# Both norms of a one-layer decoder trunk handed to TensorE chunk by chunk, with filler transposes and a first weight slot in halves

## The chip, the cores and the metric

The kernel runs on one core of one Trainium2 chip. The metric is the device time of a run in microseconds (us), the median of several runs. The engines are PE (TensorE: `MATMUL` and, as PEld, its weight loads), DVE (VectorE), ACT (ScalarE), POOL (GpSimd) and SP (SyncE, which here only issues DMAs). They run side by side, each through its own list of instructions in order, and meet only at semaphores.

## The reference

One layer on x, 256 tokens by 1024 channels, all float32:

```
h  = rmsnorm(x, norm1)                       # first norm
z  = h @ w_in                                # split into rx, ry, q, kc, vc, ks, vs, kw, vw, ng, mg
A  = rg_lru(causal_conv(rx)) * gelu(ry)      @ w_rg_out
B  = nsa(q, compressed / selected / window keys and values, sigmoid(ng)) @ w_nsa_out
x1 = x + (sigmoid(mg0) * A + sigmoid(mg1) * B) @ w_o
h2 = rmsnorm(x1, norm2)                      # second norm
y  = x1 + (silu(h2 @ w_gate) * (h2 @ w_up)) @ w_down

rmsnorm(x, g) = x * rsqrt(mean(x*x over the 1024 channels) + 1e-6) * g
```

## The kernel before

Every float32 product is made of three products of a reduced float32 format: a value v is split into hi (v rounded) and lo (v - hi), and a product is hi*hi + hi*lo + lo*hi. Weights come from memory as a stream of 73 slots of 128 x 2048 float32 (1 MB each), in the order rx (4 slots), kk 2, rg 2, kc, vc, qa 2, qb 2, vv 2, ry 4, rgo 4, mg 8, nso 4, wo 4, gu 22 (gate and up), dn 11. SP loads a slot into `raw` (three buffers), ACT writes `w_hi` (`split_hi`, L360), DVE writes `w_lo` (`split_lo`, L649), then PE may use the slot (`slot_ready`). SP loads into a buffer again when DVE has finished the `w_lo` of its last slot.

Slots of 256 output columns are "direct" (L1048 to L1050: 48 matmuls of 256 columns for a slot, weights stationary, the normed activations moving), others "panel" (24 matmuls of 512 columns, same lines), and the gu slots are "wide" (L1088 and L1091: hi and lo of the activations lie side by side in `h_hl`, so that one 512-column matmul with `w_hi` and one of 256 columns with `w_lo` do the three products of a chunk). A slot has two output halves, mt = 0 and 1, each over the 8 chunks k of 128 channels.

Each norm has to turn its rows (tokens on partitions) into columns (channels on partitions) for PE. For the first norm: ACT squares rows 0 to 127 (L366), DVE rows 128 to 255 (L657), DVE makes the means (L654), POOL raises them to the power -0.5 (L332), ACT and DVE scale the rows (L369, L665), PE transposes them in four units of two chunks each, unit j into PSUM bank `misc(m)` = 4 + m % 4 (L1124), ACT writes `h_hi` with the gain (L377, `unit_hi`), DVE `h_lo` (L696, `unit_lo`), two chunks under one semaphore count. PE's first slot waits at every second chunk k of mt = 0 for the unit (`wait_misc_read`). ACT makes the whole `w_hi` of slot 0 between its scaling and its units, DVE the whole `w_lo` between its scaling and its units. After the transposes stand 24 filler transposes of the identity (`keep_busy`, L1148).

The second norm stands between wo and gu, in the iterations FIRST["wo"] + 3 and + 4 of the three engines' loops. The residual sum x1 is made in two panels of 512 columns (L996 for the first, L1009 for the second, one instruction for each half t of the tokens). ACT squares each panel half with an accumulator (L613), DVE joins the two sums (L1001, L1011), POOL makes the power (L332), DVE scales rows t = 0 and half of t = 1 (L1015), ACT the other half (L620), PE transposes t = 0, then t = 1 (L1405), and `unit_hi` and `unit_lo` (L377, L696) hand over to the first gu slot. No fillers stand there.

The order of the work is written out by hand: each engine has one loop over the slots.

Of the kernel before, what the change touches and what calls it, by code (L numbers as in the profile page):

```python
# [87 lines left out]
def hybrid_layer(nc, x, stream, small_w, params, out):  # L88
    ctx = ExitStack()
    with ctx:  # L90
# [119 lines left out]
        squares, ms_ready, rs_ready = sem("squares"), sem("ms_ready"), sem("rs_ready")  # L210
        evac_hi = sem("evac_hi")
# [58 lines left out]
        def _(sp):  # L270
# [5 lines left out]
            for r in range(RAW):  # L276
                load(r, r)
# [71 lines left out]
        def _(sc):  # L349
# [22 lines left out]
            def unit_hi(m, j, gain_col):  # L372

                sc.wait_ge(misc_done, misc_count(m))
                for e in range(2):
                    c = 2 * j + e
                    ins = sc.activation(h_hi[:, c, :], misc(m)[:, e * S:(e + 1) * S], ACT.Copy,  # L377
                                        scale=prm[:, gain_col + c:gain_col + c + 1])
                ins.then_inc(evac_hi, 1)
# [30 lines left out]
            for i in range(NSLOT + 2):  # L410
# [197 lines left out]
                for pnl in range(2):  # L608
                    if i == FIRST["wo"] + pnl + 3:
                        for t in range(T2):  # L610
                            sc.wait_ge(x1_ready, 2 * pnl + t + 1)
                            c = 2 * pnl + t
                            sc.activation(scr[:, 512 * c:512 * (c + 1)], xs[:, t, pnl * 512:(pnl + 1) * 512], ACT.Square,  # L613
                                          accum_out=ss[:, NORM_X1, c:c + 1]).then_inc(squares, 1)
                            if (pnl, t) == (1, 0):
                                split_hi(i + AHEAD - 1)
                if i == FIRST["wo"] + 4:
# [3 lines left out]
                    for j in range(4):  # L621
                        unit_hi(MISC["hT2"] + j, j, G2)
# [13 lines left out]
        def _(ve):  # L636
# [29 lines left out]
            split_lo(0)  # L666
# [25 lines left out]
            def unit_lo(m, j, gain_col, count):  # L692
                ve.wait_ge(evac_hi, count)
                for e in range(2):
                    c = 2 * j + e
                    ins = ve.scalar_tensor_tensor(out=h_lo[:, c, :], in0=misc(m)[:, e * S:(e + 1) * S],  # L696
                                                  scalar=prm[:, gain_col + c:gain_col + c + 1],
                                                  in1=f(h_hi[:, c, :]), op0=ALU.mult, op1=ALU.subtract)
                ins.then_inc(misc_free[m % 4], 1)

            for j in range(4):
                unit_lo(MISC["xT"] + j, j, G1, j + 1)
            ve.wait_ge(small_hi, 1)
            ve.tensor_tensor(sw_lo[:, :], smraw, f(sw_hi[:, :]), ALU.subtract).then_inc(small_lo, 1)
            split_lo(1)
# [13 lines left out]
            def q_lo(pnl):  # L719

                for v in range(2):
                    m = MISC[("qTa", "qTb")[pnl]] + v
                    pr = 4 * pnl + 2 * v
                    ve.wait_ge(evac_hi, 8 + 2 * pnl + v + 1)
# [7 lines left out]
            for i in range(NSLOT + 2):  # L732
# [25 lines left out]
                if i == HEAD0:  # L758
                    q_lo(1)
                    u = USE["kcT"]  # L760
                    ve.wait_ge(evac_hi, 13)
# [119 lines left out]
                if i == FIRST["kk"] + 4:  # L881
                    for g in range(GROUPS):
                        m = MISC["kT"] + g
                        ve.wait_ge(evac_hi, 4 + g + 1)
# [97 lines left out]
                for v in range(2):  # L982
                    if i == FIRST["wo"] - 1 + 2 * v:
                        for j in (2 * v, 2 * v + 1):
                            m = MISC["mT"] + j
                            ve.wait_ge(evac_hi, 13 + j + 1)
# [16 lines left out]
                if i == FIRST["wo"] + 4:  # L1003
                    for t in range(T2):
# [4 lines left out]
                        ve.tensor_tensor(xs[:, t, 512:1024], acc(USE["wo"] + 2 + t)[:, :], xs[:, t, 512:1024], ALU.add).then_inc(x1_ready, 1)  # L1009
                        ve.wait_ge(squares, 11 + t)  # L1010
                        ve.tensor_scalar(ms[:, NORM_X1, t:t + 1], ss[:, NORM_X1, 2 + t:3 + t], 1.0 / D, ss[:, NORM_X1, 4 + t:5 + t],  # L1011
# [33 lines left out]
        def _(pe):  # L1045
# [108 lines left out]
            for j in range(4):  # L1154
                transposed_unit(MISC["xT"] + j, xn, j)
# [329 lines left out]
```

## Time and profile before

| | us |
|---|---|
| timed runs | 503.60, 501.64, 503.51 (median 503.51) |
| profiled execution, its own time | 501.95 |
| its span, first to last instruction | 500.2 |
| PE busy | 485.0 (97% of the span) |
| DVE busy | 335.0 (67%) |
| ACT busy | 285.5 (57%) |
| POOL busy | 15.0 (3%) |

1.75 us of the profiled execution lie outside its span. A busy engine is one with an instruction in flight; since PE's matmuls overlap (a 256-column matmul is shown as 0.28 us, while the next starts 0.12 us later), PE's pace is read from the distance of the starts, not from the durations.

### The profile page before, as it was taken

The page shows a single profiled execution, that of the slowest core. Times are in us where ns is not written, and L with a number is a line of the kernel's source. Part 1 is how long each engine was busy: PE and PEld are TensorE (multiplying, and loading weights), DVE is VectorE, ACT ScalarE, POOL GpSimd, SP SyncE. Part 2 cuts the span into 40 slices and gives each one's busy share as a digit, 9 for nine tenths or more (in the row PEclk, how much of TensorE's full clock was granted, in tenths as well). Part 3 has the DMA queues.
Part 4 walks back from the last instruction along what each step waited for, and adds up shares of the span by engine and source line. Part 5 has one row for each costly group of instructions (what it writes and reads, how often), then busy time and mean ns, then how long its engine had stood idle before and what let it go on. Part 6 is the DMA issues. An engine that isn't in the chain of part 4 may idle for free.

```text
span 500.2 us, 7322 instructions
## 1 busy us (share of the span) xinstructions
PE 485.0 (97%) x2849; PEld 417.8 (84%) x2849; DVE 335.0 (67%) x504; ACT 285.5 (57%) x453; POOL 15.0 (3%) x24
## 2 busy tenths in 40 slices
PE   6999999999999989999999997999999999999997
PEld 5998998788988768878787886888888888888885
DVE  2999699788876576657663764766666666654432
ACT  5646786676478777675673336555545554553330
POOL 2000200220000000000000000000000000000000
PEclk9999999999999999999999998899999999999999
DMA  8655777424222444243335362455554554465402
GB/s 334 241 168 210 287 282 277 168 85 168 85 85 86 168 169 168 91 163 105 148 137 197 97 244 85 168 178 203 210 169 172 201 216 170 174 211 204 169 0 84
DMA packets 12544, 84.72 MB, mean 169 GB/s; under 512 B 1504, under 2 KB 1504, under 8 KB 2656
## 3 DMA queue, kind: packets, MB, share of 16 engines
q1 hardware_dynamic: 11808, 82.32, 45.2%
q0 software_dynamic: 272, 1.05, 0.7%
q10 hardware_dynamic: 432, 0.91, 0.5%
q8 instruction: 22, 0.36, 0.3%
q14 instruction: 10, 0.08, 0.0%
HBM read 83.22 MB, written 1.05 MB: 168 GB/s over the span
## 4 chain that ended last, share of the span: by engine, by line
PE 84%; DVE 7%; ACT 6%; issue 2%; DMA 1%; POOL 0%; POOLq 0%; DVEq 0%; ACTq 0%
PE bank L1048 17%; PE bank L1050 17%; PE bank L1049 17%; PE bank L1088 17%; PE bank L1091 9%; DVE w_lo L649 2%; ACT pbuf L446 2%; ACT w_hi L360 1%; PE bank L1337 1%; PE bank L1168 1%; DVE ast L754 1%; DMA xs<-x_dram 1%; PE bank L1179 1%; PE bank L1206 1%; PE bank L1124 1%
## 5 line engine op out<-in xcount | busy, mean ns | idle before, releaser
L649 DVE TENSOR_TENSOR w_lo<-raw,w_hi 128x2048 fp32r<-128x2048 f32 x73 | 167.1, 2291 | 73.4 <-ACT w_hi L360 73.0
L360 ACT ACTIVATE w_hi<-raw 128x2048 fp32r<-128x2048 f32 x73 | 139.6, 1915 | 49.9 <-PE bank L1050 49.9
L1088 PE MATMUL bank<-h_hl,w_hi 128*128 128x512 f32 x352 | 91.1, 397 | 0.7 <-DVE h_hl L696 0.7
L1088 PEld LDWEIGHTS bank<-h_hl,w_hi 128*128 128x128 f32 x352 | 64.4, 192 | 12.7 <-issue 1.1
L1048 PE MATMUL bank<-w_hi,h_hl 128*128 128x512 f32 x160 | 63.5, 397 | 0.0
L1050 PE MATMUL bank<-w_hi,h_hl 128*128 128x512 f32 x160 | 62.4, 390 | 0.0
L1049 PE MATMUL bank<-w_lo,h_hl 128*128 128x512 f32 x160 | 62.4, 390 | 0.0
L1048 PE MATMUL bank<-w_hi,act 128*128 128x512 f32 x152 | 59.9, 394 | 2.5 <-DVE act L797 2.5
L1050 PE MATMUL bank<-w_hi,act 128*128 128x512 f32 x152 | 59.2, 390 | 0.0
L1049 PE MATMUL bank<-w_lo,act 128*128 128x512 f32 x152 | 59.2, 389 | 0.0
L1091 PEld LDWEIGHTS bank<-h_hl,w_lo 128*128 128x128 f32 x352 | 49.6, 194 | 3.4
L1091 PE MATMUL bank<-h_hl,w_lo 128*128 128x256 f32 x352 | 51.0, 285 | 0.0
L1048 PE MATMUL bank<-h_hl,w_hi 128*128 128x256 f32 x160 | 46.0, 288 | 0.4 <-DVE h_hl L696 0.4
L479 ACT ACTIVATE scr<-bank 128x512 f32<-128x512 f32 x22 | 13.2, 599 | 58.1 <-PE bank L1088 58.1
L1050 PE MATMUL bank<-h_hl,w_lo 128*128 128x256 f32 x160 | 45.2, 283 | 0.0
L1049 PE MATMUL bank<-h_hl,w_hi 128*128 128x256 f32 x160 | 45.2, 283 | 0.0
L446 ACT ACTIVATE pbuf<-bank,ast 128x128 f32<-128x128 f32 (+1 forms) x64 | 26.1, 420 | 19.2 <-DVE ast L757 19.2
L1048 PEld LDWEIGHTS bank<-w_hi,act 128*128 128x128 f32 x152 | 28.5, 188 | 8.9 <-DVE act L797 3.0
L1050 PEld LDWEIGHTS bank<-w_hi,h_hl 128*128 128x128 f32 x160 | 30.0, 188 | 6.4
L1048 PEld LDWEIGHTS bank<-w_hi,h_hl 128*128 128x128 f32 x160 | 30.1, 188 | 6.2 <-issue 0.4
L1049 PEld LDWEIGHTS bank<-w_lo,h_hl 128*128 128x128 f32 x160 | 30.1, 188 | 5.8
L1050 PEld LDWEIGHTS bank<-w_hi,act 128*128 128x128 f32 x152 | 28.5, 188 | 6.1
(213 smaller groups left out, 678.6 us busy)
## 6 DMA issues: line engine op xcount, KB each, us to landing
raw<-stream_dram SPq DMA_DIRECT2D x73, 1024.0 KB, 4.8
w<-stream_dram SPq DMA_DIRECT2D x4, 1024.0 KB, 8.5
xs<-x_dram POOLq DMA_DIRECT2D x1, 1024.0 KB, 5.4
out_dram<-xs SPq DMA_DIRECT2D x4, 256.0 KB, 2.0
xs<-x_dram ACTq DMA_DIRECT2D x1, 512.0 KB, 5.2
xs<-x_dram SPq DMA_DIRECT2D x1, 512.0 KB, 5.0
scr<-small_dram ACTq DMA_DIRECT2D x1, 320.0 KB, 10.3
prm<-params_dram ACTq DMA_DIRECT2D x1, 58.0 KB, 7.5
```

Of the source, the lines that this page charges most:

```text
L360: sc.activation(w_hi[:, i % HL, :], raw[:, i % RAW, :], ACT.Copy).then_inc(hi_ready, 1)
L446: ins = sc.activation(prob[:, a:b], bank[:, off:off + b - a], ACT.Exp, bias=ast[:, 1, j:j + 1], scale=SCALE, accum_out=ast[:, 2, j:j + 1])
L479: sc.activation(gus[:, j % 2, :, :], gate_up(j)[:, :, S:2 * S], ACT.Copy).then_inc(gu_low, 1)
L649: ve.tensor_tensor(w_lo[:, i % HL, :], raw[:, i % RAW, :], f(w_hi[:, i % HL, :]), ALU.subtract).then_inc(lo_ready, 1)
L754: ins = ve.tensor_reduce(ast[:, 0, 2 * t:2 * t + 2], misc(m + t)[:, 0:2 * w].rearrange("p (b c) -> p b c", b=2), AX, ALU.max)
L1048: pe.matmul(out_, l_hi, r_hi, start=start, stop=False)
L1049: pe.matmul(out_, l_hi, r_lo, start=False, stop=False)
L1050: return pe.matmul(out_, l_lo, r_hi, start=False, stop=stop)
L1088: ins = pe.matmul(acc(u + mt)[:, :], w_hi[:, s, c:c + P], a_hl[:, k, :, :].rearrange("p x s -> p (x s)"), start=k == 0, stop=k == KC - 1)
L1091: ins = pe.matmul(acc(u + mt)[:, 0:S], w_lo[:, s, c:c + P], a_hl[:, k, 0, :], start=False, stop=False)
L1124: ins = pe.transpose(misc(m)[:, e * S + t * P:e * S + (t + 1) * P], src[:, t, c * P:(c + 1) * P], ident[:, :])
L1168: pe.matmul(o3, q, kt[:, g, :].rearrange("p (b c) -> p b c", b=2)[:, :, 0:w], start=n == 0, stop=n == 1)
```

## The change

The slot loads, the weight split of slot 0, both handovers and the statistics of the second norm's second panel change; the reference and the arithmetic of the products stay. The wide gate and up slots stay as they are, but for what they wait for.

```diff
@@ sync
-            for r in range(RAW):
+            for e in range(2):
+                sp.dma_start(raw[:, 0, e * 1024:(e + 1) * 1024], stream[0, :, e * 1024:(e + 1) * 1024]).then_inc((first_half, landed[0])[e], 16)
+            for r in range(1, RAW):
                 load(r, r)
@@ scalar
             sc.activation(xsq, xs[:, 0, :], ACT.Square, accum_out=ss[:, NORM_X, 0:1]).then_inc(squares, 1)
+            sc.wait_ge(first_half, 16)
+            sc.activation(w_hi[:, 0, 0:1024], raw[:, 0, 0:1024], ACT.Copy).then_inc(hi_half, 1)
             sc.wait_ge(rs_ready, rs_count(NORM_X))
             sc.wait_ge(x1_in, 16)
             sc.activation(xn[:, 1, :], xs[:, 1, :], ACT.Copy, scale=rs[:, NORM_X, 1:2]).then_inc(xn1_ready, 1)
-            split_hi(0)
+            sc.wait_ge(landed[0], 16)
+            sc.activation(w_hi[:, 0, 1024:2048], raw[:, 0, 1024:2048], ACT.Copy).then_inc(hi_ready, 1)
+            def chunks_hi(unit, norm, gain_col):
+                for c in range(KC):
+                    m = unit + c % 4
+                    if c < 4:
+                        sc.wait_ge(misc_done, misc_count(m))
+                    else:
+                        sc.wait_ge(h_lo_ready, KC * norm + c - 3)
+                    sc.activation(h_hi[:, c, :], misc(m)[:, c // 4 * S:(c // 4 + 1) * S], ACT.Copy,
+                                  scale=prm[:, gain_col + c:gain_col + c + 1]).then_inc(h_hi_ready, 1)
             sc.wait_ge(prm_in, 16)
-            for j in range(4):
-                unit_hi(MISC["xT"] + j, j, G1)
+            chunks_hi(MISC["xT"], 0, G1)
+            split_hi(1)
             sc.wait_ge(small_in, 16)
             sc.activation(sw_hi[:, :], smraw, ACT.Copy).then_inc(small_hi, 1)
-            split_hi(1)
@@ scalar, i == FIRST["wo"] + pnl + 3
-                            sc.wait_ge(x1_ready, 2 * pnl + t + 1)
-                            c = 2 * pnl + t
-                            sc.activation(scr[:, 512 * c:512 * (c + 1)], xs[:, t, pnl * 512:(pnl + 1) * 512], ACT.Square,
-                                          accum_out=ss[:, NORM_X1, c:c + 1]).then_inc(squares, 1)
-                            if (pnl, t) == (1, 0):
+                            if pnl == 0:
+                                sc.wait_ge(x1_ready, t + 1)
+                                sc.activation(scr[:, 512 * t:512 * (t + 1)], xs[:, t, 0:512], ACT.Square,
+                                              accum_out=ss[:, NORM_X1, t:t + 1]).then_inc(squares, 1)
+                            elif t == 0:
                                 split_hi(i + AHEAD - 1)
...
-                    for j in range(4):
-                        unit_hi(MISC["hT2"] + j, j, G2)
+                    chunks_hi(MISC["hT2"], 1, G2)
@@ vector
-            split_lo(0)
+            ve.wait_ge(hi_half, 1)
+            ve.tensor_tensor(w_lo[:, 0, 0:1024], raw[:, 0, 0:1024], f(w_hi[:, 0, 0:1024]), ALU.subtract)
+            ve.wait_ge(hi_ready, 1)
+            ve.tensor_tensor(w_lo[:, 0, 1024:2048], raw[:, 0, 1024:2048], f(w_hi[:, 0, 1024:2048]), ALU.subtract).then_inc(lo_ready, 1)
...
+            def chunks_lo(unit, norm, gain_col):
+                for c in range(KC):
+                    m = unit + c % 4
+                    ve.wait_ge(h_hi_ready, KC * norm + c + 1)
+                    ve.scalar_tensor_tensor(out=h_lo[:, c, :], in0=misc(m)[:, c // 4 * S:(c // 4 + 1) * S],
+                                            scalar=prm[:, gain_col + c:gain_col + c + 1],
+                                            in1=f(h_hi[:, c, :]), op0=ALU.mult, op1=ALU.subtract).then_inc(h_lo_ready, 1)
+                for j in range(4):
+                    ve.wait_ge(h_lo_ready, KC * norm + j + 5)
+                    ve.engine_nop().then_inc(misc_free[(unit + j) % 4], 1)
...
@@ vector, i == FIRST["wo"] + 4
-                        ve.wait_ge(squares, 11 + t)
-                        ve.tensor_scalar(ms[:, NORM_X1, t:t + 1], ss[:, NORM_X1, 2 + t:3 + t], 1.0 / D, ss[:, NORM_X1, 4 + t:5 + t],
-                                         ALU.mult, ALU.add).then_inc(ms_ready, 1)
+                        ve.wait_ge(x1_ready, 3 + t)
+                        ve.tensor_tensor_reduce(out=scr[:, 1024 + 512 * t:1536 + 512 * t], in0=xv, in1=xv, scale=1.0 / D,
+                                                scalar=ss[:, NORM_X1, 4 + t:5 + t], op0=ALU.mult, op1=ALU.add,
+                                                accum_out=ms[:, NORM_X1, t:t + 1]).then_inc(ms_ready, 1)
@@ tensor, direct() and wide(), the first slot behind a norm
-                        if units is not None and mt == 0 and k % 2 == 0:
-                            wait_misc_read(pe, units + k // 2)
+                        if norm is not None and mt == 0:
+                            pe.wait_ge(h_lo_ready, KC * norm + k + 1)
@@ tensor, first norm (each unit now holds the chunks j and j + 4)
-                transposed_unit(MISC["xT"] + j, xn, j)
-            keep_busy(24)
+                ...
+                        c = 4 * e + j
+                ...
+            keep_busy(8)
@@ tensor, second norm
                     pe.wait_ge(xn_ready, 2)
+                    u = USE["wo"]
+                    pe.wait_ge(acc_free[u % 4], u // 4 + 1)
+                    def idle_busy(n):
+                        for _ in range(n):
+                            pe.transpose(acc(u)[:, 0:P], ident[:, :], ident[:, :])
                     for t in range(T2):
+                        if t == 1:
+                            idle_busy(10)
+                            pe.wait_ge(xn_ready, 3)
+                            pe.wait_ge(xn1_ready, 2)
                         for j in range(4):
...
-                            elif j == 0:
-                                pe.wait_ge(xn_ready, 3)
-                            elif j == 2:
-                                pe.wait_ge(xn1_ready, 2)
...
+                    idle_busy(5)
```

The counts of the semaphore `evac_hi` that later users wait for fall by 4 (8 behind the second norm), since the norms no longer raise it.

ACT's list at the start, before and then of the changed kernel. `h_hl` is the pair of `h_hi` and `h_lo`, `sw_hi` the small weights.

```order
5 L366 ACTIVATE scr,ss<-xs 128x1024
6 L369 ACTIVATE scr<-xs,rs 128x1024
7 L360 ACTIVATE w_hi<-raw 128x2048
8 L377 ACTIVATE h_hl<-bank,prm 128x256 x8
9 L385 ACTIVATE sw_hi<-scr 128x640
10 L360 ACTIVATE w_hi<-raw 128x2048 x2
```

```order
5 L370 ACTIVATE scr,ss<-xs 128x1024
6 L372 ACTIVATE w_hi<-raw 128x1024
7 L375 ACTIVATE scr<-xs,rs 128x1024
8 L377 ACTIVATE w_hi<-raw 128x1024
9 L387 ACTIVATE h_hl<-bank,prm 128x256 x8
10 L364 ACTIVATE w_hi<-raw 128x2048
11 L394 ACTIVATE sw_hi<-scr 128x640
```

Half of slot 0's `w_hi` moves ahead of the scaling of the rows, and the small weights move behind slot 1.

DVE's list between the second panel of x1 and the first gu slot, before and then changed. The changed kernel's L1021 is the residual sum, L1023 the new reduction (listed as ISA, with the read of its accumulator behind it), L1028 the scaling.

```order
274 L1009 TENSOR_TENSOR xs<-bank,xs 128x512
275 L1011 TENSOR_SCALAR ms<-ss 128x1
276 L1015 TENSOR_SCALAR scr<-xs,rs 128x1024
277 L1009 TENSOR_TENSOR xs<-bank,xs 128x512
278 L1011 TENSOR_SCALAR ms<-ss 128x1
279 L1015 TENSOR_SCALAR scr<-xs,rs 128x512
```

```order
276 L1021 TENSOR_TENSOR xs<-bank,xs 128x512
277 L1023 ISA scr,ms<-xs,ss 128x512
278 L1023 ISA ms 128x1
279 L1028 TENSOR_SCALAR scr<-xs,rs 128x1024
280 L1021 TENSOR_TENSOR xs<-bank,xs 128x512
281 L1023 ISA scr,ms<-xs,ss 128x512
282 L1023 ISA ms 128x1
283 L1028 TENSOR_SCALAR scr<-xs,rs 128x512
```

The squares of the second panel now stand on DVE itself, where before it waited for ACT's.

PE's list at the second norm, before and then changed. The rows with `ident,scr` are the transposes of the norm, those with `ident` alone the fillers.

```order
1459 L1405 MATMUL bank<-ident,scr 128x128 x16
1460 L1088 MATMUL bank<-h_hl,w_hi 128x512
```

```order
1459 L1430 MATMUL bank<-ident,scr 128x128 x8
1460 L1417 MATMUL bank<-ident 128x128 x10
1461 L1430 MATMUL bank<-ident,scr 128x128 x8
1462 L1417 MATMUL bank<-ident 128x128 x5
```

Ten fillers stand between the transposes of t = 0 and t = 1, five between those and the first gu slot.

## Rows read from the trace of the kernel before

**Rows 1.** The page, busy engines and the chain that ended last.

```profile
PE 485.0 (97%) x2849; PEld 417.8 (84%) x2849; DVE 335.0 (67%) x504; ACT 285.5 (57%) x453; POOL 15.0 (3%) x24
...
PE 84%; DVE 7%; ACT 6%; issue 2%; DMA 1%; POOL 0%; POOLq 0%; DVEq 0%; ACTq 0%
```

**Rows 2.** Timeline, start: start us, us, engine line op out<-in [idle before <-releaser].

```profile
5.86 1.06 ACT L366 ACTIVATE scr<-xs 128x1024 f32<-128x1024 f32 x1 [2.34 <-DMA xs<-x_dram]
6.04 1.22 DVE L657 SCALAR_TENSOR_TENSOR scr<-xs 128x1024 f32<-128x1024 f32 x1 [6.04 <-DMA xs<-x_dram]
...
8.31 1.15 ACT L369 ACTIVATE scr<-xs,rs 128x1024 f32<-128x1024 f32 x1 [1.31 <-POOL rs L332]
...
9.37 1.90 ACT L360 ACTIVATE w_hi<-raw 128x2048 fp32r<-128x2048 f32 x1
...
9.61 1.94 PE L1124 MATMUL bank<-ident,scr 128*128 128x128 f32 x16 [1.89 <-ACT scr L369]
11.18 3.00 ACT L377 ACTIVATE h_hl<-bank,prm 128x256 fp32r<-128x256 f32 x8
...
11.30 2.29 DVE L649 TENSOR_TENSOR w_lo<-raw,w_hi 128x2048 fp32r<-128x2048 f32 x1 [2.23 <-ACT w_hi L360]
11.38 2.78 PE L1148 MATMUL bank<-ident 128*128 128x128 f32 x24
13.51 3.22 DVE L696 SCALAR_TENSOR_TENSOR h_hl<-bank,prm,h_hl 128x256 fp32r<-128x256 f32 x8
...
14.53 0.36 PE L1048 MATMUL bank<-h_hl,w_hi 128*128 128x256 f32 x1 [0.37 <-DVE h_hl L696]
...
17.38 2.29 DVE L649 TENSOR_TENSOR w_lo<-raw,w_hi 128x2048 fp32r<-128x2048 f32 x1
...
20.48 0.28 PE L1048 MATMUL bank<-h_hl,w_hi 128*128 128x256 f32 x1
```

**Rows 3.** DMA issues, slot 0's load, issued at 1.27: size, us to landing.

```profile
raw<-stream_dram SPq DMA_DIRECT2D x1, 1024.0 KB, 7.3
```

**Rows 4.** Busy time, 20 to 52: PE, PEld, DVE, ACT, POOL, clock, DMA.

```profile
20.00:52.00 32.00, 32.00 (x226) 29.92 (x225) 30.50 (x63) 16.24 (x19) 0.00 (x0) 1.00 0.61 223
```

**Rows 5.** Timeline, second norm.

```profile
304.30 0.63 ACT L613 ACTIVATE scr<-xs 128x512 f32<-128x512 f32 x1 [1.45 <-DVE xs L1009]
...
305.37 0.56 POOL L332 TENSOR_TENSOR rs<-ms,half 128x1 f32<-128x1 f32 x1 [126.48 <-DVE ms L1011]
...
308.99 0.72 ACT L620 ACTIVATE scr<-xs,rs 128x512 f32<-128x512 f32 x1 [0.91 <-POOL rs L332]
...
309.53 1.68 PE L1405 MATMUL bank<-ident,scr 128*128 128x128 f32 x8 [1.67 <-DVE scr L1015]
...
310.01 3.03 ACT L377 ACTIVATE h_hl<-bank,prm 128x256 fp32r<-128x256 f32 x8 [0.30 <-PE bank L1405]
...
310.88 3.22 DVE L696 SCALAR_TENSOR_TENSOR h_hl<-bank,prm,h_hl 128x256 fp32r<-128x256 f32 x8 [1.41 <-ACT h_hl L377]
...
311.90 0.77 PE L1088 MATMUL bank<-h_hl,w_hi 128*128 128x512 f32 x1 [0.69 <-DVE h_hl L696]
...
314.02 4.48 DVE L649 TENSOR_TENSOR w_lo<-raw,w_hi 128x2048 fp32r<-128x2048 f32 x2
...
319.95 0.60 ACT L479 ACTIVATE scr<-bank 128x512 f32<-128x512 f32 x1 [5.11 <-PE bank L1088]
```

**Rows 6.** Windows of PE: us, PE busy (instructions), granted clock, DMA share, GB/s.

```profile
309.00:309.50 0.50, 0.00 (x0) 1.00 0.00 0
...
310.00:310.50 0.50, 0.50 (x4) 0.50 0.00 0
...
316.50:317.00 0.50, 0.50 (x4) 0.79 0.00 0
```

**Rows 7.** Chain of waits in a later gu slot: start us, us, what.

```profile
325.73 0.95 PE bank L1091 x8
326.68 1.84 PE bank L1088 x8
```

More of the change, by code:

```diff
@@ L690, in softplus @@
                 ve.tensor_scalar(sm[:, 11, :], prm[:, BI:BI + 8], 0.5, None, ALU.mult).then_inc(sp_ready, 1)
[L692 to L702, printed above, removed]
+            def chunks_lo(unit, norm, gain_col):
[8 more added lines that the diff above has]
+                    ve.engine_nop().then_inc(misc_free[(unit + j) % 4], 1)
+            chunks_lo(MISC["xT"], 0, G1)
+            split_lo(1)
             ve.wait_ge(small_hi, 1)
             ve.tensor_tensor(sw_lo[:, :], smraw, f(sw_hi[:, :]), ALU.subtract).then_inc(small_lo, 1)
-            split_lo(1)
             ve.wait_ge(consts, 4)
@@ L1019, in _ @@
                     ve.engine_nop().then_inc(acc_free[USE["even"] % 4], 1)
-                    for j in range(4):
-                        unit_lo(MISC["hT2"] + j, j, G2, 17 + j + 1)
+                    chunks_lo(MISC["hT2"], 1, G2)
                 j = i - FIRST["gu"] - 1
@@ L1053, in slot_ready, with direct @@
                 pe.wait_ge(lo_ready, i + 1)
-            def direct(i, u, a_h, a_l, units=None, between=None):
+            def direct(i, u, a_h, a_l, norm=None, between=None):
                 slot_ready(i)
@@ L1069, in direct, with wide @@
                 ins.then_inc(slot_done, 1)
-            def wide(i, u, a_hl, units=None):
+            def wide(i, u, a_hl, norm=None):
                 slot_ready(i)
@@ L1078, in wide @@
                     low = [("lo", k) for k in range(KC)]
-                    if units is not None and mt == 0:
+                    if norm is not None and mt == 0:
                         order = [high[0]] + [low[0]] + [z for k in range(1, KC) for z in (low[k], high[k])]
@@ L1083, in wide @@
                     for part, k in order:
-                        if units is not None and mt == 0 and k % 2 == 0:
-                            wait_misc_read(pe, units + k // 2)
+                        if norm is not None and mt == 0:
+                            pe.wait_ge(h_lo_ready, KC * norm + k + 1)
                         c = k * 256 + mt * P
@@ L1154, in _ @@
             for j in range(4):
-                transposed_unit(MISC["xT"] + j, xn, j)
-            keep_busy(24)
+                m = MISC["xT"] + j
+                wait_misc_free(pe, m)
+                for e in range(2):
+                    for t in range(T2):
+                        c = 4 * e + j
+                        ins = pe.transpose(misc(m)[:, e * S + t * P:e * S + (t + 1) * P], xn[:, t, c * P:(c + 1) * P], ident[:, :])
+                ins.then_inc(misc_done, 1)
+            keep_busy(8)
             def scores(h):
@@ L1245, in _ @@
                     if 0 <= r < dict(ORDER)[name]:
-                        units = {FIRST["rx"]: MISC["xT"]}.get(i)
-                        direct(i, USE_RY[r] if name == "ry" else USE[name] + r, h_hi, h_lo, units,
+                        norm = {FIRST["rx"]: 0}.get(i)
+                        direct(i, USE_RY[r] if name == "ry" else USE[name] + r, h_hi, h_lo, norm,
                                compressed_transposed if i == HEAD0 + 2 else None)
```

24 lines of the change are left out of this document (10 added, 14 removed).

## The prediction

> **What bounds the kernel now.** I read the page first: PE is busy for 97% of the span, and 84% of the chain that ended last is PE [rows 1]. So only what lets PE start sooner, stand less or run at a higher clock can move the end. Then the timeline at the two places where PE does stand, the norms. In the first [rows 2] PE stands 1.89 us for the scaling of the rows, transposes from 9.61, idles in fillers, and starts slot rx0 at 14.53, because ACT makes all of `w_hi` of slot 0 (9.37 to 11.27) before it touches a unit and DVE all of `w_lo` (11.30 to 13.59) before it makes the first `h_lo`. In the second [rows 5] PE stands before the transposes of t = 1 (1.67 us) and before the first gu slot (0.69 us); that slot starts at 311.90 and ACT can read its result at 319.95. Last the windows [rows 6]: the granted clock is 1.00 up to 309.5, 0.50 from about 309.9 (the lower of the two levels, 1.2 instead of 2.4 GHz), and comes back near 316.7. It falls just after the 1.67 us of standing and stays low for nearly 7 us of real work. At full clock a gu slot takes 2 x (0.95 + 1.84) = 5.58 us [rows 7]; from 311.90 to 319.95 are 8.05.
>
> **First norm, part by part.** Half of slot 0's `w_hi` (1024 columns, 1.06 us by L366's row of that size [rows 2]) moves to before the scaling, where ACT stands 1.31 us for POOL. ACT is free there near 7.0. The whole slot lands at 1.27 + 7.3 = 8.6 [rows 3]; x landed near 5.8, so half of the slot that follows it on the queue should be there near 7.2 to 7.3. Then ACT makes the half from 7.25 to 8.3 and the scaling starts as before at 8.31 or 0.1 later. No row shows a stream slot in two transfers: at best the half costs ACT's path nothing, at worst it lands only with the whole at 8.6, which puts the scaling, the transposes and the clock's idle stretch 1.3 us later. I take 0.05, near the first, since the queue is already moving then. The two loads behind it are issued one DMA issue later; `w_hi` of slot 1 is made only at 13.5, long after.
>
> After the scaling (to 9.5) ACT needs 1.06 instead of 1.90 for the rest of `w_hi`: to 10.5. DVE has made the first half of `w_lo` by then (half of 2.29 = 1.15, from 9.1) and the second runs from 10.5 to 11.65. Its 8 chunks, at the pitch of 3.22/8 = 0.40 [rows 2], run to 14.9 instead of 16.7. ACT's chunks start at 10.5, at 3.00/8 = 0.38 each, but the first four follow the transposes (16 at about 0.11 from 9.65: 11.55), so they end near 13.5, ahead of DVE throughout. The extra waits (8 on DVE, 4 on ACT for chunks that DVE left four chunks ago) are met when they are reached; I cost them, and the 4 empty instructions on DVE, at 0.1 together, with DVE's 0.8 of slack at slot 1 (below) as their cover.
>
> PE: transposes to 11.55, 8 fillers at 2.78/24 = 0.12 to 12.5. The first chunk is ready at 12.1, so the fillers decide by a little: rx0 starts at 12.5 instead of 14.53. It took 5.95 (14.53 to 20.48, 48 matmuls [rows 2]); its eighth chunk is wanted at 12.5 + 7 x 0.36 = 15.0 and is there at 14.9. So rx1 can start at 18.45: **2.0 us gained**. Its weights: ACT's `w_hi` of slot 1 at 13.5 to 15.4, DVE's `w_lo` to 17.7. Slack 0.8, as before (17.38 + 2.29 = 19.67 against 20.48). The small weights, now behind slot 1, are ready near 18.4, and PE wants them only after rx1, near 24.
>
> Does it carry to the end? DVE is busy for 30.5 of 32 us between 20 and 52 [rows 4] and its part of the shift there is only about 1.3 us (it now stands 0.4 for slot 1's `w_hi`). But PE does not wait for it in that stretch; the weights of slots 2 to 9 are ready 4 us or more ahead, so 0.7 of lost slack is not felt. I take all 2.0.
>
> **Second norm.** ACT's squares of the second panel (0.63 and the read of the accumulator [rows 5], with two changes of engine) become one reduction on DVE. From the end of the residual sum to POOL's start was 1.10 (304.27 to 305.37). The new instruction: the nearest row is L657, same shape of work on 1024 columns with an accumulator, 1.22 [rows 2]; for 512 that is 0.65, plus a read. With 0.15 of handing over 0.86: 0.24 less, twice on the chain (t = 0, t = 1), so 0.5. Bounds: 0.55 to 1.25 for the instruction, if it took as long as L657's whole row; that end costs 2 x 0.6 instead. ACT's freed time is used by nobody. DVE's half of the scaling ends earlier, but PE now waits for ACT's half too (0.72, [rows 5]) before its first transpose: start at 309.3 instead of 309.53.
>
> What DVE's reduction costs is also told by the Trainium skill (Vector Engine (DVE) Microarchitecture Reference, section Points that are easy to get wrong): a fused two-source instruction of this family with both sources in SBUF and not bf16 runs at half rate. L657 is such an instruction with an accumulator and took 1.22 for 1024 columns, no more than half of a 2048-column subtraction with two float32 sources (2.29 [rows 2]), so the trace speaks against it. By the rule the sum below would be 1.0 us higher.
>
> Handover: two transposes and a hand-over 0.3, one chunk on ACT 0.38, one on DVE 0.43: the first chunk is ready at 310.4, where before two chunks on each engine made it 311.8. PE runs 8 transposes and 5 fillers at 0.12 until 310.8, so the gu slot starts at 310.8. DVE's eighth chunk is ready at 310.0 + 3.22 = 313.25, and is wanted at 310.8 + 7 x 0.35 = 313.25. At full clock the slot's result is ready for ACT at 310.8 + 5.58 + 0.2 = 316.6 instead of 319.95: **3.35 us gained**, of which 1.1 is the earlier start and the rest the clock. gu1 is covered: its `w_lo` follows the chunks, 313.25 + 2.29 = 315.55 (4.48 for two [rows 5]), wanted at 316.4.
>
> Whether the clock stays up: before, PE stood 0.6, worked 1.1, stood 1.67, worked 1.3 and stood 0.69. The ten fillers take 1.1 to 1.2 of the gap between the two sets of transposes (near 307.4 to 309.3), leaving about 0.7; the last standing is filled. At the start a stand of 1.89 with work on both sides left the clock at 1.00, so a fall at 0.7 is unlikely.
>
> **Sum.** 501.95 - 2.0 - 3.35 = 496.6 for an execution like the profiled one. The executions of before fall on two levels: 501.95 and 501.64, and 503.51 and 503.60. The distance, 1.6 to 1.9, is what half the clock costs in some 3 us of PE-bound work. The stand of 1.89 in the first norm is as long as the one that cost the clock in the second, and it stays in the changed kernel; I take it that it costs the clock in some executions. The Trainium skill (TensorE: Matmul & The Clock Gate, section What's actually happening) says that the gate's counting runs free of the kernel, so that the same kernel changes its clock at other places from run to run; one trace can't show that. Since the two levels are equally frequent I add half their distance: **497.4**.
>
> **Rivals.** *The clock falls in the second norm all the same.* For it: standing of 0.5 and 0.7 remains, with transposes, not full matmuls, between. Then 13 transposes and fillers at 0.21 end at 312.1, and with the low clock up to 316.7 [rows 6] the slot ends at about 319.7: the gain is 0.2, the time 499.8 (to 501.4 on the upper level). Chance 0.10.
>
> *The first half lands late or the shift gets lost.* With the half at 8.6, PE transposes at 10.8, DVE's second half ends at 13.1, the chunks at 16.3, rx0 ends near 19.55: gain 0.95. Or DVE's full stretch [rows 4] holds PE up by the 0.7. Time 498.1 to 498.5. Chance 0.12.
>
> *The reduction runs at half rate.* By the L657 row taken whole: t = 1 comes 1.2 later, PE stands 1.8 again, and the clock may fall; 497.8, with the fall 501. Chance 0.04.
>
> *Slower.* The fillers at the first norm go from 24 to 8. If the clock falls at the 1.89 us of standing and, as at 309.9, does not come back for 6.8 us, transposes, fillers and rx0 run at the low level: it costs 3.4. With the clock lost in the second norm too: 501.95 - 2.0 - 0.2 + 3.4 = 503.2, slower than the profiled execution. It decides from the point where both falls happen and each lasts 6.8 us or more. Against it: the clock held at this place before, and the work behind it is now denser. Chance 0.03, and 0.02 to pass the bound below.
>
> **How the numbers follow.** Forecast 0.71, its own range 495.8 to 498.9 (0.8 for either level, 0.5 for my hand-over times). The whole range 495.2 to 499.9 takes in the late half, the slow reduction, and the fallen clock on the lower level. A measurement tells about 0.5% (2.5 us) from no change: faster is below 501.0. Forecast, lost shift and nearly all of the two clock cases are: 0.93 faster, 0.05 same, 0.02 slower.
>
> **What would show it.** In the profile after: rx0's first matmul near 12.5 and rx1's near 18.45; POOL's two powers 0.24 and 0.48 earlier relative to the last wo matmul; ACT's first read of a gu slot 3.3 us sooner relative to it; the clock at 1.00 from 306 to 320. Wrong if the clock shows 0.50 there, if the new reduction takes over 0.9, or if ACT's first half starts only near 8.3.

## The result and the profile after

| | before | changed |
|---|---|---|
| median of 7 runs each | 501.64 (501.21 to 503.60) | 499.33 (497.43 to 500.73) |
| ratio | | 0.9942, 95% interval 0.9923 to 0.9962 |
| profiled execution, its own time | 501.95 | 500.68 |
| its span | 500.2 | 499.0 |

The kernel got faster by 0.6%, and the 499.33 lies inside the range, though 1.9 above the forecast. The page of the changed kernel answers to [rows 1]:

```profile
PE 486.9 (98%) x2848; PEld 420.4 (84%) x2848; DVE 336.6 (67%) x507; ACT 284.9 (57%) x450; POOL 15.0 (3%) x24
...
PE 89%; ACT 4%; DVE 3%; DMA 1%; issue 1%; POOLq 0%; POOL 0%; SPq 0%; ACTq 0%; DVEq 0%
```

PE holds more of the chain, and with as many matmuls it is busy for longer in a shorter span. That alone says that some of its work got slower. Start to start of the slots' first matmuls tells where (read by counting matmuls: 48 for a direct slot, 24 for a panel, 32 for a gu slot; rx1 is the second rx slot, gu1 the second gu slot, wo3 the last wo slot):

| stretch | before | changed | difference |
|---|---|---|---|
| start to rx1 | 20.48 | 20.22 | -0.26 |
| rx1 to ry0 | 101.19 | 101.19 | 0.00 |
| ry0 to wo3 | 178.91 | 180.74 | +1.83 |
| wo3 to gu1 | 19.16 | 16.35 | -2.81 |
| gu1 to dn0 | 117.32 | 117.32 | 0.00 |

The first norm gave almost nothing, the second 2.8, and 1.8 were lost in between, where the change touches nothing. In all three the clock has a part. The start of the changed kernel, PE, ACT and DVE (start us, us, engine line op), against [rows 2]:

```profile
7.91 1.06 ACT L372 ACTIVATE w_hi<-raw 128x1024 fp32r<-128x1024 f32 x1 [0.93 <-DMA raw<-stream_dram]
8.87 1.13 ACT L375 ACTIVATE scr<-xs,rs 128x1024 f32<-128x1024 f32 x1
9.95 1.06 ACT L377 ACTIVATE w_hi<-raw 128x1024 fp32r<-128x1024 f32 x1
...
11.04 1.23 DVE L676 TENSOR_TENSOR w_lo<-raw,w_hi 128x1024 fp32r<-128x1024 f32 x1 [0.82 <-ACT w_hi L377]
...
10.15 3.39 PE L1172 MATMUL bank<-ident,scr 128*128 128x128 f32 x16 [1.97 <-ACT scr L375]
```

The first half of slot 0 landed at 7.9 instead of the 7.25 forecast, which made the scaling start at 8.87 instead of 8.31; and the same 16 transposes took 3.39 instead of 1.94. PE stood 1.97 us, and then the clock was low. In another profiled execution of the same kernel ("once more" below) it stood longer and the clock stayed, with rx1 at 18.79:

```profile
10.19 1.94 PE L1172 MATMUL bank<-ident,scr 128*128 128x128 f32 x16 [2.68 <-ACT scr L375]
```

Windows of PE (us, PE busy, granted clock, DMA share, GB/s), two of the first norm, three near 130, two of the second norm:

```profile
10.50:11.00 0.50, 0.50 (x5) 0.50 0.85 360
13.50:14.00 0.50, 0.50 (x5) 0.65 1.02 426
129.50:130.00 0.50, 0.50 (x6) 0.90 0.00 0
130.00:130.50 0.50, 0.50 (x4) 0.50 0.00 0
136.50:137.00 0.50, 0.50 (x5) 0.77 0.00 0
310.00:310.50 0.50, 0.32 (x3) 1.00 0.00 0
312.00:312.50 0.50, 0.50 (x6) 1.00 0.00 0
```

At half clock (1.2 GHz) from 10.4 to 13.8 and from 129.9 to 136.7; at full clock through the second norm, where [rows 6] showed 0.50. What PE does near 130, changed kernel:

```profile
127.17 1.86 PE L1401 MATMUL bank<-cmpr,act 128*128 128x32 f32 x16
...
129.08 2.67 PE L1401 MATMUL bank<-cmpr,act 128*128 128x32 f32 x16
...
131.95 1.05 PE L1197 MATMUL bank<-ident,pbuf 128*128 128x128 f32 x4
```

These are the scores of the compressed branch, 32 matmuls of only 32 columns. The kernel before issues the same ones at the same place at full clock in its profiled execution:

```profile
129.34 1.85 PE L1383 MATMUL bank<-cmpr,act 128*128 128x32 f32 x16
...
131.25 0.60 PE L1179 MATMUL bank<-ident,pbuf 128*128 128x128 f32 x4
```

Its window there, as above:

```profile
130.00:130.50 0.50, 0.50 (x7) 1.00 0.00 0
```

The profiles of the runs below settle what this fall costs. From ry0 to wo3 passed 178.9 us in the four profiled executions without a fall near 130 (the kernel before, first norm alone, 46 fillers, half behind the scaling), 179.1 in the one where it lasted 3.4 us, and 180.7 to 180.8 in eight where it lasted 6.8 us: 1.8 us. In the tenth with such a fall, where fillers had been added at this place, it was 182.5.

The second norm of the changed kernel, against [rows 5]. L1023 is the new reduction with the read of its accumulator, L1417 are the fillers:

```profile
305.87 0.75 DVE L1023 CUSTOM_DVE_ANT_0 scr<-xs,ss 128x512 f32<-128x512 f32 x1
306.55 0.08 DVE L1023 DVE_READ_ACCUMULATOR2_ANT ms<- 128x1 f32 x1
...
308.13 1.09 PE L1430 MATMUL bank<-ident,scr 128*128 128x128 f32 x8 [0.38 <-DVE scr L1028]
309.06 1.25 PE L1417 MATMUL bank<-ident 128*128 128x128 f32 x10
311.01 1.06 PE L1430 MATMUL bank<-ident,scr 128*128 128x128 f32 x8 [0.69 <-ACT scr L628]
...
311.45 3.03 ACT L387 ACTIVATE h_hl<-bank,prm 128x256 fp32r<-128x256 f32 x8 [0.59 <-PE bank L1430]
...
311.96 3.23 DVE L706 SCALAR_TENSOR_TENSOR h_hl<-bank,prm,h_hl 128x256 fp32r<-128x256 f32 x8 [1.33 <-ACT h_hl L387]
...
318.70 0.60 ACT L487 ACTIVATE scr<-bank 128x512 f32<-128x512 f32 x1 [2.41 <-PE bank L1100]
```

PE stands 0.69 where it stood 1.67, and the eight transposes behind take 1.06 instead of 1.68.

### The profile page after: what moved, and what is told of

The parts are those of the page before. It is cut to its first block, busy times and chain, and to the rows that moved or that the text cites. A ratio compares the mean times of both kernels' runs of the same rounds, so it can differ in the third digit from the quotient of the medians.

```text
span 499.0 us, 7330 instructions
## 1 busy us (share of the span) xinstructions
PE 486.9 (98%) x2848; PEld 420.4 (84%) x2848; DVE 336.6 (67%) x507; ACT 284.9 (57%) x450; POOL 15.0 (3%) x24
## 4 chain that ended last, share of the span: by engine, by line
PE 89%; ACT 4%; DVE 3%; DMA 1%; issue 1%; POOLq 0%; POOL 0%; SPq 0%; ACTq 0%; DVEq 0%
PE bank L1060 18%; PE bank L1061 18%; PE bank L1062 18%; PE bank L1100 16%; PE bank L1103 8%; PE bank L1186 2%; PE bank L1197 1%; PE bank L1355 1%; DVE w_lo L656 1%; DMA raw<-stream_dram 1%; ACT pbuf L454 1%; PE bank L1224 1%; ACT w_hi L364 1%; PE bank L1401 1%; DVE ast L765 1%
## 5 line engine op out<-in xcount | busy, mean ns | idle before, releaser
L656 DVE TENSOR_TENSOR w_lo<-raw,w_hi 128x2048 fp32r<-128x2048 f32 x72 | 164.8, 2291 | 72.2 <-ACT w_hi L364 71.7
L364 ACT ACTIVATE w_hi<-raw 128x2048 fp32r<-128x2048 f32 x72 | 137.8, 1915 | 46.0 <-PE bank L1062 45.8
L1100 PE MATMUL bank<-h_hl,w_hi 128*128 128x512 f32 x352 | 89.3, 392 | 0.0
L1100 PEld LDWEIGHTS bank<-h_hl,w_hi 128*128 128x128 f32 x352 | 63.3, 189 | 11.2 <-issue 0.2
L1103 PEld LDWEIGHTS bank<-h_hl,w_lo 128*128 128x128 f32 x352 | 48.4, 190 | 4.0
L454 ACT ACTIVATE pbuf<-bank,ast 128x128 f32<-128x128 f32 (+1 forms) x64 | 26.1, 420 | 13.8 <-DVE ast L768 13.7
```

What stands on the lines that cost most here:

```text
L364: sc.activation(w_hi[:, i % HL, :], raw[:, i % RAW, :], ACT.Copy).then_inc(hi_ready, 1)
L454: ins = sc.activation(prob[:, a:b], bank[:, off:off + b - a], ACT.Exp, bias=ast[:, 1, j:j + 1], scale=SCALE, accum_out=ast[:, 2, j:j + 1])
L656: ve.tensor_tensor(w_lo[:, i % HL, :], raw[:, i % RAW, :], f(w_hi[:, i % HL, :]), ALU.subtract).then_inc(lo_ready, 1)
L1100: ins = pe.matmul(acc(u + mt)[:, :], w_hi[:, s, c:c + P], a_hl[:, k, :, :].rearrange("p x s -> p (x s)"), start=k == 0, stop=k == KC - 1)
L1103: ins = pe.matmul(acc(u + mt)[:, 0:S], w_lo[:, s, c:c + P], a_hl[:, k, 0, :], start=False, stop=False)
```

## The experiments

Every execution comes with its span and mean granted clock. Sorted by that clock, the 79 executions of the kernel before that ran beside the experiments fall into four groups: 15 at 1.00 (median 499.71), 37 at 0.993 (501.32), 11 at 0.990 (501.79), 16 at 0.986 (503.47). A mean of 0.993 is what one low stretch of 6.8 us makes, as in the first trace. So the kernel before is itself between 499.5 and 503.7, nearly all of it by the clock, and what an edit is worth can be read apart from it: among executions at 1.00. In the table "at 1.00" is the median of those, "mean" that over all executions of a kernel (kernel before: 501.55). "Clock theory" below is the view that the time is lost to the granted clock and not to the handover.

| kernel | executions | mean | at 1.00 (number) | ratio to before, 95% |
|---|---|---|---|---|
| changed, both sets | 13 | 498.69 | 497.43 (3) | 0.9923 to 0.9962; 0.9896 to 0.9952 |
| second norm alone | 12 | 499.65 | 498.94 (5) | 0.9938 to 0.9978 |
| first norm alone | 12 | 500.72 | 498.23 (3) | 0.9964 to 1.0012 |
| before + fillers | 12 | 500.15 | 499.69 (4) | 0.9956 to 0.9990 |
| changed, no fillers in second norm | 12 | 499.01 | 497.48 (1) | 0.9935 to 0.9973 |
| changed, 46 fillers at the start | 6 | 498.02 | 497.75 (1) | 0.9903 to 0.9958 |
| changed, squares on ACT | 10 | 498.92 | 497.81 (6) | 0.9928 to 0.9973 |
| changed, half behind the scaling | 6 | 497.96 | 497.69 (5) | 0.9908 to 0.9956 |
| changed, small weights later | 6 | 497.92 | 497.18 (3) | 0.9902 to 0.9952 |
| changed, handover by units | 6 | 498.97 | 498.41 (3) | 0.9924 to 0.9967 |
| changed, fillers at the compressed scores | 12 | 499.75 | 497.87 (2) | 0.9934 to 0.9978 |
| three edits together | 7 | 498.18 | 497.14 (4) | 0.9894 to 0.9951 |

**The second norm's part alone.** The kernel before with chunks_hi and chunks_lo, the reduction, the joint wait and the fillers in the second norm only.

```diff
-                    for j in range(4):
-                        unit_hi(MISC["hT2"] + j, j, G2)
+                    chunks_hi(MISC["hT2"], 0, G2)
...
+                            idle_busy(10)
```

> The kernel before with the second norm's part alone (squares on DVE, fillers, chunk handover, wait for both halves). Clock theory: the clock stays at 1.00 through the second norm, from wo3's first matmul to gu1's are 16.4 us instead of 19.2, and the time falls by about 2.8 us against before. Rival (the second norm gives little, the first norm made the difference): under 1.5 us.

16.35 from wo3 to gu1, the clock theory's number. But the mean fell by 1.9, not by 2.8: at clock 1.00 only 0.8 is gained (499.71 to 498.94), and the rest comes only against executions in which the clock fell there. Its profiled execution (500.87) had the fall near 130.

**The first norm's part alone.** The changed kernel with the second norm of before.

```diff
-                    chunks_hi(MISC["hT2"], 1, G2)
+                    for j in range(4):
+                        unit_hi(MISC["hT2"] + j, j, G2)
...
-                            idle_busy(10)
```

> The changed kernel with the second norm as before. Clock theory: the first norm gives 1.2 to 2.0 us where the clock holds over PE's standing at 8 to 10 us, and 0.3 where it falls there, so the median is 0.3 to 1.5 below before, with two levels. Rival (the late landing of the first half, 7.9 instead of 7.25, takes the whole gain, clock or not): no level more than 0.5 below before.

At 1.00 it gains 1.5 (499.71 to 498.23), against the rival, although the half lands as late as in the changed kernel. Its profiled execution kept the clock at the first norm:

```profile
7.85 1.06 ACT L372 ACTIVATE w_hi<-raw 128x1024 fp32r<-128x1024 f32 x1 [0.92 <-DMA raw<-stream_dram]
...
10.10 1.94 PE L1190 MATMUL bank<-ident,scr 128*128 128x128 f32 x16 [1.40 <-ACT scr L375]
...
12.70 0.36 PE L1078 MATMUL bank<-h_hl,w_hi 128*128 128x256 f32 x1
```

The half starts at the same 7.9, the transposes take 1.94 instead of 3.39, and rx0 starts at 12.70 instead of 14.38, rx1 at 18.69. That execution also kept the clock in the unchanged second norm: wo3 to gu1 took 17.17. So the 19.16 of before are 17.2 of work and waiting and 2.0 of low clock. Over all executions nothing can be told from no change: 6 of 12 had a mean of 0.986 or lower. That PE stood 1.67 before the second norm's last transposes here too, as in the kernel before, and kept the clock, shows that the length of the standing alone doesn't decide.

**No fillers in the second norm.**

```diff
-                            idle_busy(10)
...
-                    idle_busy(5)
```

> The changed kernel without the 10 and 5 fillers of the second norm. Clock theory: PE stands about 1.8 us again, the clock falls to 0.50 for 6.8 us in most executions, and 1.5 to 2 us of the 2.8 are given back (median 1 to 2 above the changed kernel). Rival (the handover by chunks and the reduction on DVE are what gained): same as the changed kernel within 0.5, or 0.4 faster, as no filler stands before the first gu slot.

Both expectations were half right. PE stood 1.78 us and the clock fell, but for 3.4 us instead of 6.8 (windows of PE; the transposes took 1.94):

```profile
308.50:309.00 0.50, 0.00 (x0) 1.00 0.00 0
309.00:309.50 0.50, 0.10 (x1) 0.54 0.00 0
312.00:312.50 0.50, 0.50 (x3) 0.55 0.00 0
312.50:313.00 0.50, 0.50 (x4) 1.00 0.00 0
```

wo3 to gu1 took 16.90, only 0.55 more than with fillers, and the mean over executions 499.01, 0.3 more, within the spread. What the fillers are worth in the changed kernel is therefore not shown by its time; by the profiles, the clock fell in the second norm in two of the three executions without fillers there (not in that of the first norm alone) and in none of the eleven with them.

**The kernel before with the fillers alone.**

```diff
+                        if t == 1:
+                            for _ in range(10):
+                                pe.transpose(acc(u)[:, 0:P], ident[:, :], ident[:, :])
...
+                    for _ in range(5):
+                        pe.transpose(acc(u)[:, 0:P], ident[:, :], ident[:, :])
```

> The kernel before with the 10 and 5 fillers in its second norm, and nothing else of the change. Theory (what the change gains there beyond its handover is the clock, which fell in the kernel before because PE stood 1.67 us): the clock stays up, from wo3's first matmul to gu1's are 17.2 us instead of 19.2, at mean clock 1.00 the time is the 499.7 of the kernel before, and the mean over executions falls by 1.2 to 1.6 since the fall there was in three of four. Rival (the clock was kept by the handover and the reduction, which shorten the standing; the fillers do nothing, as without them the changed kernel was no slower): the levels 0.993 to 0.986 stay as frequent as before and the mean falls by less than 0.5.

This tells the clock from the handover, in the kernel before. The 0.986 and 0.990 groups vanish, 2 of 12 are at 0.992 (of before 27 of 79 are at 0.990 or below and 37 at 0.993), at 1.00 nothing moves (499.69), and the mean falls by 1.4. Its second norm, PE:

```profile
306.94 1.09 PE L1410 MATMUL bank<-ident,scr 128*128 128x128 f32 x8 [0.59 <-DVE scr L1015]
307.87 1.25 PE L1399 MATMUL bank<-ident 128*128 128x128 f32 x10
309.70 1.09 PE L1410 MATMUL bank<-ident,scr 128*128 128x128 f32 x8 [0.57 <-DVE scr L1015]
```

wo3 to gu1 took 17.18, the value of the unfallen clock above. The rival fell.

**More fillers at the start.** 46 instead of 28.

```diff
-            keep_busy(28)
+            keep_busy(46)
```

> The changed kernel with 46 instead of 28 fillers at the start, so that PE is busy up to the first transposes. Clock theory: no fall at the first norm in any execution; rx0 starts near 12.9 to 13.1 instead of 14.4, and the median is 0.8 to 1.5 below the changed kernel (499.3). Rival (late landing alone): rx0 near 14.4 as now and the same time, or 0.3 slower by fillers that hold the transposes up.

No fall at the first norm in its profiled execution. But the fillers ran to about 10.9 and made PE's transposes late (10.78 instead of 10.1), so that at 1.00 it takes 497.75. Six executions, none above 499.20: the top group is gone, for 0.3 in the others. rx0 started at 13.32, later than the 12.9 to 13.1 expected, and the median of 497.82 is 1.5 below the 499.33, but 1.0 below the median of all 13 executions of the changed kernel. Whether the fall at the first norm is what went can't be told from six.

**Squares on ACT.** The two instructions of the reduction undone.

```diff
-                        ve.tensor_tensor_reduce(out=scr[:, 1024 + 512 * t:1536 + 512 * t], in0=xv, in1=xv, scale=1.0 / D,
+                        ve.wait_ge(squares, 11 + t)
+                        ve.tensor_scalar(ms[:, NORM_X1, t:t + 1], ss[:, NORM_X1, 2 + t:3 + t], 1.0 / D, ss[:, NORM_X1, 4 + t:5 + t],
```

> The changed kernel with the second panel's squares on ACT again (all else as changed). Theory (the reduction on DVE saves two changes of engine on the chain, but takes 0.83 instead of the forecast 0.73): 0.2 to 0.5 us slower than the changed kernel among executions of the same mean clock (497.4 at 1.00). Rival (its cost on DVE equals what it removes): the same within 0.1. PE's standing before the transposes of t = 1 grows from 0.69 to about 1.1 in the trace.

497.81 at 1.00, 0.4 more, and 16.76 from wo3 to gu1 instead of 16.35: the reduction is worth 0.4. PE stands 0.90 instead of 0.69 (1.1 was expected).

**The half behind the scaling.** ACT makes both halves of slot 0's w_hi after it has scaled the rows.

```diff
-            sc.wait_ge(first_half, 16)
-            sc.activation(w_hi[:, 0, 0:1024], raw[:, 0, 0:1024], ACT.Copy).then_inc(hi_half, 1)
             sc.wait_ge(rs_ready, rs_count(NORM_X))
...
+            sc.wait_ge(first_half, 16)
+            sc.activation(w_hi[:, 0, 0:1024], raw[:, 0, 0:1024], ACT.Copy).then_inc(hi_half, 1)
             sc.wait_ge(landed[0], 16)
```

> The changed kernel with ACT's first half of slot 0's w_hi made behind the scaling of the rows, so that nothing of the scaling waits for the slot. Theory (the early half is worth about half a us, since it lands only at 7.9 and pushes the scaling from 8.3 to 8.9): PE's first transpose at 9.6 instead of 10.1, DVE's eighth chunk at 16.1 instead of 15.3, 0.4 to 0.8 slower than the changed kernel at the same mean clock. Rival (the late half costs all that it gives): the same or faster, since the clock's idle stretch is 0.5 shorter.

497.69 at 1.00, 0.26 more (expected 0.4 to 0.8), so the early half is worth little; that its late landing is the reason is argued, not shown. PE's transposes start at 9.51 and PE then waits for DVE's first chunk until 13.25. The standing is 0.56 here, and 5 of 6 executions are at 1.00. That would fit a clock that falls by the length of the standing. But in four other profiles with slot 0 in halves PE stood 2.49 (small weights later), 2.63 (units), 2.68 (changed, again) and 2.90 us (squares on ACT) and the clock stayed at 1.00, so it doesn't show it.

**Small weights later.**

```diff
-            sc.dma_start(smraw, small_w[:, :]).then_inc(small_in, 16)
...
             sc.activation(w_hi[:, 0, 0:1024], raw[:, 0, 0:1024], ACT.Copy).then_inc(hi_half, 1)
+            sc.dma_start(smraw, small_w[:, :]).then_inc(small_in, 16)
```

> The changed kernel with the small weights' load issued by ACT after the first half of w_hi instead of at the start. Theory (the 320 KB of small weights share the 16 DMA engines with slot 0 and delay its first half): the half lands near 7.3 to 7.5 instead of 7.9, the scaling starts 0.4 to 0.5 sooner, and the kernel gains 0.2 to 0.5. Rival (the half's landing is set by the row size or by the queue behind x): landing still at 7.8 to 7.9, same time.

The rival's landing: the DMA issues show the first half, issued at 1.27, landing after 6.5 us, in the changed kernel after 6.6. The second half did gain: it landed at 9.1 instead of 9.9, but ACT came to it only at 9.8.

```profile
raw<-stream_dram SPq DMA_DIRECT2D x1, 512.0 KB, 6.5
```

At clock 1.00 it takes 497.18, 0.25 less, on three executions of each; where from, the runs don't show. rx1 started at 18.62, and among the other kernels with the changed start it did so at 18.59 to 18.79 where the clock stayed and the half landed by 7.9.

**Handover by units** of two chunks in both norms, the rest as changed.

```diff
-            chunks_hi(MISC["xT"], 0, G1)
+            for j in range(4):
+                unit_hi(MISC["xT"] + j, j, G1)
...
-                            pe.wait_ge(h_lo_ready, KC * norm + k + 1)
+                            wait_misc_read(pe, units + k // 2)
```

> The changed kernel with the handover by units of two chunks in both norms, as before (halved slot 0, fillers and reduction as changed). Theory (the chunks bring PE's start forward by about 0.8 in each norm, but DVE's last chunk sets the end of the slot and comes only 0.4 later by units): 0.3 to 0.8 slower than the changed kernel at the same mean clock. Rival (the handover is the gain at full clock): 1.5 or more slower.

498.41 at 1.00, 1.0 more, above the 0.3 to 0.8 expected: 17.05 from wo3 to gu1 instead of 16.35 (0.7); the other 0.3 is left for the first norm, where the half landed 0.35 later in this profile, so its trace can't price the chunks there. The chunks are the largest part of the gain at full clock, 1.0 of 2.3.

**The changed kernel once more.**

> The changed kernel once more, unchanged, for the spread over its clock levels. Theory (free of the kernel, the clock's changes fall at other places from execution to execution): levels at 497.3 to 497.5 (clock 1.00), near 497.7 to 498.8 (0.997), 499.4 (0.993) and 500.7 (0.989), none that shows a fall in the second norm; the median lies anywhere from 497.5 to 499.5. Rival (the 499.33 is a fixed cost of the change): 499.3 again within 0.3.

497.72 for the median of six, against 499.33 of seven before: 497.35 and 497.75 at 1.00, 497.61 and 497.69 at 0.996, 499.22 and 499.25 at 0.993. Of the 13 together the median is 498.83. The rival fell: the 499.33 is a draw from these groups.

**Fillers at the compressed scores**, 8 ahead of each group of 16.

```diff
                         wait_acc_free(pe, u)
+                        for _ in range(8):
+                            pe.transpose(acc(u)[:, 0:P], ident[:, :], ident[:, :])
```

> The changed kernel with 8 filler transposes ahead of each of the two groups of compressed scores (16 matmuls of 32 columns each, at 127 to 131). Theory (the stretch of 32-column matmuls is what costs the clock 6.8 us near 130 in some executions, 1.9 to 2.2 us each time): the levels 0.993 and 0.989 vanish or get rare; the fillers themselves cost 0 to 1.7 us at clock 1.00, depending on how long PE waits there for ACT and DVE. Rival (the fall there comes from what stands ahead or behind): the levels stay as frequent, about one execution in three.

No better: the mean is 1.1 above that of the changed kernel, though the intervals overlap. The levels did not vanish, as the rival said: 6 of 12 executions are at 0.997 and 499.45, 4 at 0.993 and 501.17, and the fall near 130 remains in the profiled one. At 1.00 the fillers cost 0.4. Fillers ahead of a thin stretch didn't keep the clock up, and a fall there is paid by more PE work (182.5 from ry0 to wo3 instead of 180.7).

**Three edits together**: small weights later, 38 fillers at the start, none behind the second norm's transposes.

```diff
+            keep_busy(38)
...
-                    idle_busy(5)
```

> The changed kernel with three edits that the runs so far favour: the small weights' load later, 38 instead of 28 fillers at the start, and none behind the transposes of the second norm. Theory: at clock 1.00 it takes 497.0 to 497.2, no execution has the fall at the first norm, and the median is about 0.3 below that of the same kernel with 28 fillers. Rival (the five last fillers hold the clock up): falls in the second norm come back and the median rises to 498.5.

497.14 at 1.00, the lowest beside 497.18 of the small weights alone, median 498.20. No group but 1.00 and 0.993 is seen, and the profiled fall is the one near 130. The clock fell in neither norm in that execution, against the rival. Faster than before by 0.5 to 1.1%; from the changed kernel its ratio can't be told apart.

## Why the prediction came out as it did

The direction, the places and the mechanism of the second norm were right; the time was 1.9 too low against the seven runs, 1.4 against the median of all 13.

*First norm, 2.0 forecast.* Right at full clock: rx1 at 18.69 against 20.48 is 1.8, and 1.5 by the executions at 1.00. It came with an error inside: the half landed at 7.9, not 7.25, since I read half of slot 0's landing as half the time between x and the whole slot. Slot 0's second half came at 9.9, where before the whole came at 8.6 [rows 3]; ACT came to it at 9.95 and did not wait. In the execution that was profiled the clock took 1.4 of the gain (rx1 at 20.22, and at 18.79 in the other profile of the same kernel).

*Does it carry?* Yes. rx1 to ry0 took 101.2 in all kernels, though DVE's lead fell more than the 0.7 forecast: its `w_lo` of slot 2 was ready 0.45 sooner (21.77 instead of 22.22) where rx1 started 1.7 sooner. DVE's busy stretch [rows 4] did not hold PE up.

*Second norm, 3.35 forecast, 2.81 measured.* The clock's share was 2.0 (19.16 to 17.17), the handover's 0.8 (17.17 to 16.35). Taken out alone, the reduction costs 0.4 and the chunks 0.7; the two don't add up to the 0.8, and how they share it the runs don't show. The mis-sized terms are three small ones, counted from wo3's first matmul. The transposes of t = 1 began 0.15 later than forecast. From the first of them to ACT's first chunk 0.44 passed (311.01 to 311.45), not 0.3, and from there to DVE's first 0.51, not 0.38. So DVE's chunks came 0.4 late, and the first gu slot, which waits for them, took 5.90 and not 5.58. The reduction was sized well: from the end of the residual sum to POOL's start 0.89 passed, where 0.86 was forecast. The half rate that the Trainium skill gives for such an instruction (Vector Engine (DVE) Microarchitecture Reference, Points that are easy to get wrong) is not there: 0.75 for 512 columns is only 0.06 above a plain residual sum of that size (0.69).

*The sum.* This is the step that failed. I took the 2.0 of the clock as a part of every execution of before. It is absent in at least the 15 of 79 at clock 1.00, and the fillers alone, which remove it, brought the mean down by 1.4. The clock is also lost elsewhere, before and after: the executions of before lost 1.8 us to it on average (501.55 against 499.71 at 1.00), those of the changed kernel still 1.3 (498.69 against 497.43). So the change gave 2.3 at full clock and only 0.6 of clock.

*The two levels of before.* I put them down to the 1.89 us at the first norm and added half their distance. The distance fits another place better: the compressed scores near 130, which I did not name. The trace of the changed kernel shows both falls; the one near 130 cost 1.8 (ry0 to wo3, 178.91 to 180.74), and it is in ten of the fourteen profiled executions of all kernels, the one at the first norm in one. That the 0.986 group of the kernel before is this fall beside that of the second norm is inferred from the sizes, since none of those executions was profiled. At clock 1.00 the changed kernel takes 497.4, not 496.6. That the forecast has the same digits is luck: it was meant for the mean over the clock's levels, and that is 498.7.

*Rivals.* The clock's fall in the second norm was in neither profiled execution of the changed kernel. The late half came true in part (0.6 late, not 1.3). The slow reduction did not. The double fall came true at another place, the fall at the first norm cost 1.4 and not 3.4 (it lasted 3.4 us, not 6.8), and the kernel was not slower.

## What to carry to other kernels

Before an edit is priced, ask of several executions what the clock did in each, by mean clock and time, and compare executions of the same clock: here the spread by clock was 4 us, more than the edit. A handover is worth cutting to the smallest piece that the next engine can start with (1.0 us here for two norms); a filler on an engine that stands anyway cost nothing (499.69 against 499.71 at clock 1.00) and gave 1.4 us on average in the kernel before, while in the changed kernel its worth was lost in the spread (0.3); but ahead of work that is itself on the path it cost more than it kept. A load cut in two ahead of the critical step should be timed in the trace before work is queued behind its first half.

## What the runs showed of the hardware

The clock changed at places that moved between executions of one kernel, and the low stretches that ended while PE still had work lasted 3.4 or 6.8 us in all traces here. That the gate's counting runs free of the kernel, as the Trainium skill says (TensorE: Matmul & The Clock Gate, What's actually happening), agrees with this: in two executions of the changed kernel the same 16 transposes took 3.39 after 1.97 us of standing and 1.94 after 2.68. A longer standing did not make the fall likelier here: it followed 1.67, 1.78 and 1.97 us, and did not follow 1.67 in another kernel, nor 2.49 to 2.90.

Not only standing goes ahead of a fall: PE had no gap for more than 10 us before the low stretch near 130. In nine of the ten profiles that have it, it began while the 32 matmuls of 32 columns ran, and in the tenth 0.8 us behind them. That these narrow matmuls are its cause is inferred from the place; no run took them out.

Two transfers of 512 KB on one queue landed at 7.7 to 8.2 and 9.7 to 10.2 in nine profiles, where one of 1 MB in their place landed at 8.4 to 8.6 in three. With the small weights loaded later, the second of the two landed at 9.1 to 9.2 in both profiles, and the first no sooner than in the others (7.8 and 7.9).
